# Prompt retention in tile-sized chunks with a running state on VectorE, and group normalisation applied by ScalarE

## The reference

```python
def retention_block(q, k, v, S, log_gamma):
    ...
    scores = jnp.einsum("blhd,bmhd->bhlm", q, k) * decay[None]
    intra = jnp.einsum("bhlm,bmhe->blhe", scores, v)
    ...
    cross = jnp.einsum("blhd,bhde->blhe", q, S) * q_decay[None, :, :, None]
    ...
    S_new = (jnp.exp(L * log_gamma)[None, :, None, None] * S
             + jnp.einsum("blhd,blhe->bhde", k * k_decay[None, :, :, None], v))
    return intra + cross, S_new
```

## Time and profile before

| | |
|---|---|
| time, 3 runs | 1494.13 to 1495.31 us, median 1494.76 us |
| the profiled execution's own time | 1495.21 us |
| its span in the trace | 1493.2 us |
| PE busy | 1459.1 us, 98% of the span |
| DVE busy | 1016.7 us, 68% |
| ACT busy | 615.6 us, 41% |

### The profile page before, as it was taken

The page is one execution under the profiler, slowest core; times in us unless marked ns, Lnnn a source line. Parts: engine busy times, 40 slices in busy tenths (PEclk is TensorE's granted clock), DMA queues, the critical chain, the costliest instruction groups (busy, mean ns, idle before and its releaser), DMA issues. The chain is left out here.

```text
span 1493.2 us, 29385 instructions
## 1 busy us (share of the span) xinstructions
PE 1459.1 (98%) x11053; PEld 1402.9 (94%) x11053; DVE 1016.7 (68%) x1977; ACT 615.6 (41%) x1072; POOL 43.6 (3%) x83
## 2 busy tenths in 40 slices
PE   8999999999999999999999999999999999999998
PEld 7998888999999999999999988898989999999998
DVE  5347764779998349995542777457799973699832
ACT  4223444345555115553332244444365541355411
POOL 0101100000000000000010011000000000000000
PEclk9999999999999999999999999999999999999999
DMA  4523311232333323333242143112333422333322
GB/s 143 157 70 114 95 57 54 81 97 70 86 84 95 97 75 86 100 89 97 67 141 85 57 121 92 49 56 82 85 86 85 112 78 78 85 103 95 87 86 76
DMA packets 225824, 132.72 MB, mean 89 GB/s; under 512 B 4664, under 2 KB 220656, under 8 KB 225728
## 3 DMA queue, kind: packets, MB, share of 16 engines
q1 hardware_dynamic: 220624, 114.11, 27.0%
q0 software_dynamic: 5008, 17.29, 3.8%
q10 hardware_dynamic: 96, 0.02, 0.0%
HBM read 123.23 MB, written 8.18 MB: 88 GB/s over the span
## 5 line engine op out<-in xcount | busy, mean ns | idle before, releaser
L1639 PE MATMUL ps<-act,hi_down 128*128 128x288 f32 x1408 | 245.1, 296 | 0.0
L1639 PE MATMUL ps<-mix,hi_of 128*128 128x288 f32 x1280 | 225.9, 299 | 4.8 <-DVE lo_of L983 4.2
L1771 PE MATMUL ps<-mix,hi_of 128*128 128x288 f32 x1024 | 211.3, 300 | 0.0
L1639 PEld LDWEIGHTS ps<-act,hi_down 128*128 128x128 f32 x1408 | 207.2, 189 | 0.0
L1639 PEld LDWEIGHTS ps<-mix,hi_of 128*128 128x128 f32 x1280 | 188.9, 190 | 7.8 <-issue 2.9
L1771 PEld LDWEIGHTS ps<-mix,hi_of 128*128 128x128 f32 x1024 | 162.6, 188 | 10.0 <-issue 6.6
L2044 PE MATMUL ps<-sums_b,hi_S 128*128 128x288 f32 x704 | 144.5, 298 | 9.4 <-DVE p_f L1464 8.8
L841 ACT ACTIVATE hi_S<-sum_S 128x512 fp32r<-128x512 f32 x176 | 110.0, 632 | 104.5 <-PE ps L2044 79.9
L1771 PE MATMUL ps<-mix,lo_of 128*128 128x288 f32 x512 | 150.8, 295 | 0.0
L1639 PE MATMUL ps<-act,lo_down 128*128 128x288 f32 x704 | 150.7, 296 | 0.0
L2044 PE MATMUL ps<-sums_a,hi_S 128*128 128x288 f32 x704 | 143.4, 296 | 0.0
(11 more groups left out here) (236 smaller groups left out, 2693.7 us busy)
## 6 DMA issues: line engine op xcount, KB each, us to landing
raw_of<-in_w_in SPq DMA_DIRECT2D x56, 512.0 KB, 3.7
raw_down<-in_w_down SPq DMA_DIRECT2D x32, 704.0 KB, 4.6
pair_raw<-in_w_gate SPq DMA_DIRECT2D x42, 512.0 KB, 4.0
pair_raw<-in_w_up SPq DMA_DIRECT2D x42, 512.0 KB, 5.2
raw_of<-in_w_out SPq DMA_DIRECT2D x16, 512.0 KB, 4.2
strip_even<-bias_lines POOLq DMA_DIRECT2D x8, 320.0 KB, 5.2
strip_odd<-bias_lines POOLq DMA_DIRECT2D x8, 320.0 KB, 5.5
stage<-in_x_prompt SPq DMA_DIRECT2D x4, 512.0 KB, 5.9
```

The costliest lines, as they stand in the source:

```text
L1639: last = nc.tensor.matmul(ps[:, bank + half, 0:HALF], weights(w, slot, nk)[:, k, :], src[:, k, part, HALF * half:HALF * half + HALF], star ...
L1771: last = nc.tensor.matmul(ps[:, half_bank(i), 0:HALF], weights(w, n % 2, KD)[:, k, :], mix[:, k, part, HALF * half:HALF * half + HALF], st ...
```

## The change

The prompt retention is computed in chunks of one tile. Each tile has only the score product with itself (4 full and one short per head); what comes from earlier tiles goes through a state: PE makes four separate state products (`ps[:, 3, ...]`), DVE adds them up with a decay (`running_states`), and `ret_values` adds for tiles 1 to 3 a product of decayed queries (`qd`, made by DVE in `query_decay`) with the running state `s_run`. The mask of a head shrinks to one tile and is loaded for all heads in one DMA. Key decay is the same for all prompt tiles, and ACT copies the four in one instruction. DVE makes scale `gni` and offset `gnb` of the group normalisation (`group_factors`), and ACT applies them (`group_normalise`, activation Identity); a dummy Sqrt (`sqrt_table`) is put where ACT should load that table. The order of all three engines in the stage is new.

```diff
+        dmask = place("dmask", [P, HR, 2 * P], F32, A_S2 + RING * STRIP * 4)
...
+                    c = C_KDEC + h
+                    nc.scalar.activation(kd_tok[:, h % 2, 0:QT, :], ps[:, 0, :].rearrange("p (t n) -> p t n", t=QT), ACT.Copy,
+                                         scale=cst[:, c:c + 1])
+                    nc.scalar.activation(kd_tok[0:DEC, h % 2, QT, :], ps[0:DEC, 1, 0:P], ACT.Copy,
+                                         scale=cst[0:DEC, c + HR:c + HR + 1]).then_inc(kd_evac, 1)
+
+                def group_normalise(h):
+                    eng.wait_ge(gn_inv, HR * l + h + 1)
+                    if h >= RING:
+                        eng.wait_ge(or_ps, HR * l + h - 1)
                     for t in range(TT):
-                        bank, c = (0, P * t) if t < QT else (1, 0)
-                        last = nc.scalar.activation(kd_tok[0:rows(t), h % 2, t, :], ps[0:rows(t), bank, c:c + P], ACT.Copy,
-                                                    scale=cst[0:rows(t), C_KDEC + HR * t + h:C_KDEC + HR * t + h + 1])
-                    last.then_inc(kd_evac, 1)
+                        r = rows(t)
+                        last = nc.scalar.activation(o_tok[0:r, h % 2, t, :], ret_tile(t), ACT.Identity,
+                                                    scale=gni[0:r, t:t + 1], bias=gnb[0:r, t:t + 1])
+                    last.then_inc(gn_normed, 1)
+
+                def sqrt_table():
+
+                    nc.scalar.activation(spare[:], cst[:, C_ONE:C_ONE + 1], ACT.Sqrt)
...
-                for k in range(NR + 3):
-                    h, i = k // TT, k % TT
-                    if k in AT_R:
...
+                attn_out(PAIRS - 1)
+                ret_keys(0)
+                eng.wait_ge(ka_out, 32 * l + 32)
+                for t in range(TT):
+                    tok_copy(l, 2, vr, t)
+                sqrt_table()
+                for h in range(HR):
+                    if h:
                         ret_keys(h)
...
+                        group_root(h - 1)
+                    half_unit(FIRST_R + 2 * h)
+                    if h:
+                        group_normalise(h - 1)
...
-                    if i == 2 and h >= 1:
-                        group_root(h - 1)
+                        sqrt_table()
+                for p in range(PAIRS):
+                    attn_hi(p)
+                group_root(HR - 1)
+                ret_hi(0)
+                group_normalise(HR - 1)
                 gate_silu_of(HR - 1)
+                for h in range(1, HR - 1):
+                    ret_hi(h)
+                unit_hi(FIRST_OUT + 1)
                 ret_hi(HR - 1)
-
...
+                def mask_scores(h):
+
+                    dve.wait_ge(r_ps, HR * l + h + 1)
+                    if h >= RING:
+                        dve.wait_ge(sv_done, HR * l + h - 1)
+                    nc.vector.tensor_tensor(p_ret[:, h % 2, 0:SEQ].rearrange("p (t n) -> p t n", t=QT),
+                                            ps[:, 2, :].rearrange("p (t n) -> p t n", t=QT), prompt_rows(dmask[:, h, 0:P], QT), ALU.mult)
+                    nc.vector.tensor_tensor(p_ret[0:DEC, h % 2, SEQ:TOK], ps[0:DEC, 7, SPARE:SPARE + DEC], dmask[0:DEC, h, 0:DEC],
...
+                    nc.vector.tensor_tensor(qd[:, h % 2, 0:SEQ - P].rearrange("p (t n) -> p t n", t=QT - 1),
+                                            qk_ret[:, h, P:SEQ].rearrange("p (t n) -> p t n", t=QT - 1),
+                                            prompt_rows(dmask[:, h, P:2 * P], QT - 1), ALU.mult)
+                    nc.vector.tensor_tensor(qd[:, h % 2, SEQ - P:TOK - P], qk_ret[:, h, SEQ:TOK], dmask[:, h, P:P + DEC],
...
+                def running_states(h):
+
+                    step = float(gamma(h) ** P)
+                    dve.wait_ge(st_ps, HR * l + h + 1)
+                    if h >= RING:
+                        dve.wait_ge(sv_done, HR * l + h - 1)
+                    added = [ps[:, 3, DR * t:DR * t + DR] for t in range(QT)]
+                    run = s_run[:, h % 2]
+                    done = 3 * HR * l + 3 * h
+                    nc.vector.tensor_copy(run[:, 0, :], added[0]).then_inc(s_ran, 1)
+                    for t in range(1, QT):
+                        dve.wait_ge(s_ran, done + t)
+                        dst = run[:, t, :] if t + 1 < QT else st_tmp[:, 0, :]
+                        last = nc.vector.scalar_tensor_tensor(dst, run[:, t - 1, :], step, added[t], ALU.mult, ALU.add)
+                        if t + 1 < QT:
+                            last.then_inc(s_ran, 1)
...
+                def group_factors(h):
                     dve.wait_ge(gn_root, HR * l + h + 1)
                     nc.vector.reciprocal(gni[:, 0:QT], gnr[:, 0:QT])
...
+                    nc.vector.reciprocal(gni[0:DEC, QT:TT], gnr[0:DEC, QT:TT]).then_inc(gn_recip, 1)
+                    dve.wait_ge(gn_recip, HR * l + h + 1)
+                    nc.vector.scalar_tensor_tensor(gnb[:, 0:QT], mv[:, 0:QT, 0], -1.0, gni[:, 0:QT], ALU.mult, ALU.mult)
+                    nc.vector.scalar_tensor_tensor(gnb[0:DEC, QT:TT], mv[0:DEC, QT:TT, 0], -1.0, gni[0:DEC, QT:TT],
+                                                   ALU.mult, ALU.mult).then_inc(gn_inv, 1)
...
-                for k in range(NR + 4):
-                    h, i = k // TT, k % TT
...
+                query_decay(0)
+                for h in range(HR):
+                    mask_scores(h)
+                    half_unit(FIRST_R + 2 * h)
+                    if h:
+                        group_factors(h - 1)
+                    running_states(h)
+                    if h:
+                        gated(h - 1)
+                    states(h)
+                    if h + 1 < HR:
+                        query_decay(h + 1)
+                    half_unit(FIRST_R + 2 * h + 1)
+                    if h + 1 < HR:
+                        group_stats(h)
+                for p in range(2):
+                    attn_lo(p)
+                group_stats(HR - 1)
+                for p in range(2, PAIRS):
+                    attn_lo(p)
+                group_factors(HR - 1)
+                for h in range(HR - 1):
+                    gated_lo(h)
+                unit_lo(FIRST_OUT + 1)
...
+                def ret_scores(h):
+
+                    if h:
+                        pe.wait_ge(decayed, HR * l + h)
+                        pe.wait_ge(evacuated, U_LAYER * l + U_IN - HR + h + EV)
+                    for t in range(TT):
+                        dst = ps[:, 2, tok(t)] if t < QT else ps[0:DEC, 7, SPARE:SPARE + DEC]
+                        last = nc.tensor.matmul(dst, qk_ret[:, 4 + h, tok(t)], qk_ret[:, h, tok(t)], start=True, stop=True)
...
+                        pe.wait_ge(st_sum, HR * l + h)
+                    v = vr[:, :, DR * h:DR * h + DR]
+                    for t in range(QT):
+                        last = nc.tensor.matmul(ps[:, 3, DR * t:DR * t + DR], kd_tok[:, h % 2, t, :], v[:, t, :], start=True, stop=True)
+                    last.then_inc(st_ps, 1)
...
+                def dec_states(h):
+
+                    pe.wait_ge(half_out, UNITS_H * l + UNITS_H - HR + h + 1)
+                    nc.tensor.matmul(ps[:, 6, SPARE:SPARE + DR], kd_tok[0:DEC, h % 2, QT, :], vr[0:DEC, QT, DR * h:DR * h + DR],
+                                     start=True, stop=True).then_inc(dec_st_ps, 1)
...
+                def ret_values(h):
+                    pe.wait_ge(decayed, HR * l + h + 1)
+                    pe.wait_ge(qd_ready, HR * l + h + 1)
...
+                    pe.wait_ge(s_ran, 3 * HR * l + 3 * h + 3)
...
+                        out = ps[:, 4, tok(t)]
+                        nc.tensor.matmul(out, p_ret[:, h % 2, tok(t)], v[:, t, :], start=True, stop=t == 0)
+                        if t:
+                            nc.tensor.matmul(out, qd[:, h % 2, P * (t - 1):P * t], s_run[:, h % 2, t - 1, :], start=False, stop=True)
+                    out = ps[0:DEC, 5, 0:P]
+                    nc.tensor.matmul(out, qd[:, h % 2, SEQ - P:TOK - P], s_in[:, h, :], start=True, stop=False)
+                    nc.tensor.matmul(out, p_ret[0:DEC, h % 2, SEQ:TOK], v[0:DEC, QT, :], start=False, stop=True).then_inc(sv_done, 1)
...
+                ret_scores(0)
+                to_tokens(l, 2, vt)
+                for h in range(HR):
+                    if h:
                         ret_keys(h)
-                    if k < NR:
...
+                        ret_scores(h)
+                        pe.wait_ge(st_sum, HR * l + h)
+                    else:
+                        pe.wait_ge(tok_evac, 3 * TT * l + 3 * TT - 1)
...
+                    half_unit(FIRST_R + 2 * h)
+                    if h == 0:
...
-                    if 0 <= k - 2 < NR:
-                        ret_values(k - 2)
-                    if i == TT - 1 and h >= 1:
+                    ret_states(h)
+                    if h:
                         ret_out(h - 1)
-                    if i == TT - 1 and h < HR:
```

(28 more changed lines are left out.)

182 lines of the change are left out of this document (41 added, 141 removed).

## The result

The changed kernel takes 1513.04 us in the median of four runs (1507.59 to 1515.38), the kernel before beside it 1494.45: a ratio of 1.0117, with a 95% interval of 1.009 to 1.0143. It is slower by 17.5 us by that ratio (18.6 between the medians). Forecast were 1506.0 us and a range of 1495 to 1512.5: the direction is right and the forecast is 7 us too low. The measured median lies 0.5 us above the range's upper end, and the ratio applied to the 1494.76 us of the prediction gives 1512.2, right at it.

The account below looks back on a forecast made before the run. PE, busy 98% of the span, bounds the kernel: 16.0 us of products saved, but new waits make the stage +3.3 us and clock falls add 8.0. Together +11.3 on 1495.21, 1506.5, less 0.45 for the median: 1506.0 us; range 1495 to 1512.5.

Parts of the forecast that it names:

- The products saved, 16.0 us: PE in the retention: 9 products fewer a head at 0.222 us each, 8.0 us a layer, 16.0 in all.
- The wait before `ret_out`, 2.6 us in three heads: PE, heads 1 to 3: stands 2.6 us for ACT's normalised tiles, which wait for DVE's factors; 7.8 us a layer.
- five tiles in 1.38: ACT normalises a head's five tiles in 1.38 us, taken from its five decayed copies from PSUM.
- Case C: Rival: ACT's tiles take 0.4 us each, waits grow to 3.2 us, six falls, 1512.5 us; chance 0.10.
- The wait for step 5 of the tail, 3.2 us: PE in the output projection: stands 3.2 us for DVE's low part of head 1, behind ACT's table load, silu and `ret_hi(1)`.
- The last head's operand: PE in the tail, after two steps of the second unit: waits from 12.6 until 13.0 us for head 3's operand.
- The stage at the full clock, 80.2 us: Retention stage to the third unit, a layer: 61.3 + 18.9 = 80.2 us against 78.55, +1.65 a layer, +3.3 in all.
- I take five of eight at 1.6: 8.0 us: Clock on PE: five of the stage's eight new long waits are followed by a fall costing 1.6 us each, 8.0 us.
- the one known pair: Feed-forward part, both layers: PE's waits of 2.64 us, with granted clock 0.66 in the mean of the next 5 us.
- Case D: Rival: the clock falls behind every new wait, 1498.1 + 13.6 is 1511.7 us; chance 0.13.
- Case B: Rival: DVE's factors and ACT's tiles reach `ret_out` sooner, T + 2.7 instead of T + 3.7, giving 1490.1 us; chance 0.12.
- Case F: Rival: the tail's table load holds ACT for twice its 1.28 us, 2.6 us more in all, 1508.6 us; chance 0.02.

Follow-up runs that it names:

- the first experiment: Changed kernel with DVE making the previous head's normalisation factors ahead of the evacuation of a head's first half unit, not behind it: 1479.74 us, ratio 0.9922.
- the kernel at 1473.2 us: Changed kernel with DVE's factors ahead of the half unit's evacuation and ACT's high parts of heads 0 to 2 ahead of the last head's work: 1473.17 us, ratio 0.9852.

## Why the prediction was right in direction and 7 us short

- **The products saved, 16.0 us.** Right: 144 records fewer, and 8.05 us more a layer in the stage when they were put back.
- **The wait before `ret_out`, 2.6 us in three heads.** Right in place, releaser and cause, which the first experiment shows. Its size was 3.05 in all six: of the chain's links only "five tiles in 1.38" was off. ACT's tiles with scale and offset took 1.83 us; the row taken was that of copies with a scale. Case C had the direction (0.4 a tile, 2.0), and the truth lay between.
- **The wait for step 5 of the tail, 3.2 us.** Right, 3.50, the same link. The last head's operand made no wait.
- **The stage at the full clock, 80.2 us.** 79.97: the longer waits were made up by heads that are 0.25 us shorter apart from them (12.70, in the first experiment, for 12.95) and by a tail without its last wait. So this part of the sum, +3.3 in all, stands at +2.9.
- **"I take five of eight at 1.6: 8.0 us."** This is the step that failed. All eight fell, and two of them lasted twice as long: 16.45 us. The 1.6 was right for a single fall (1.7). The count was wrong, because I read the limit as lying near 2.6 us, where the one known pair was, and took the new waits to be just under it. They were 3.05 and 3.50 us, above the pair's 2.64, so the mis-sized tiles fed this step as well; and the clock fell behind six waits of 1.93 to 2.38 us too, when they were tried, so it would not have held at 2.6. Case D was this mechanism, with 0.13 and 1511.7 us; the double falls are what it lacked. The Trainium skill (TensorE: Matmul & The Clock Gate, HAM oscillation) tells of a kernel that waited some 3 to 5 us between its bursts of matmuls, and whose clock was thrown back each time. The traces agree in the heads of the changed kernel and its variants, already for shorter waits (18 of 18 of 1.93 to 3.05 us), and not in the feed-forward part, where seven of 24 of 2.60 to 2.65 us passed.
- **The sum.** 2.9 + 16.45 is 19.35 of the 20.0 us between the two spans; the stage also began 1.57 us later (242.28 for 240.71). From the end of layer 0's stage to the start of layer 1's it took 1.1 us more (653.04 for 651.91; behind its wait of 2.60 us the clock was 0.56 over 7 us, for 0.76 before), and from there to the end 2.0 less (441.49 for 443.50; no fall behind its wait of 2.64 us, for one before). None of this was in the sum, and that it nearly cancels is luck. The profiled run is also the slowest of four, which spread over 8 us (1507.59 to 1515.38) with mean clocks of 0.988 to 0.983.
- **Case B** (the factors come early) was the right place to look for a gain, and that order, with the tail's, is the kernel at 1473.2 us. **Case F**, and the drain of 1.38 us that the Trainium skill (ScalarE: Activation LUTs, What ACT_TABLE_LOAD costs) adds to a change of table: no run shows either. A load took 1.28 us with silu right behind it, and taking the early loads away cost 4.7 us where 1.28 a load gave 4.4.

## What to carry to other kernels

An engine's list decides more than its load: DVE was 66% busy and stood idle for 2.54 us right before the chain that held PE, so look for such a pair before judging an algorithm. Price a new wait on PE twice, once as a wait and once by the granted clock behind it, and let the smallest wait that fell, not the nearest one, set the count. Where a wait can't go, fill it or make it shorter, and then look at the clock again: 0.59 us left of 3.05 was enough here, 1.93 was not.

## What the runs showed of the hardware that was not expected

- **The wait's length doesn't decide alone.** Over the profiled executions of all kernels here: in the retention heads and the tail all 20 waits of 3.05 and 3.5 us and all eight of 1.93 to 2.38 were followed by a fall. Of the 24 waits of 2.60 to 2.65 us in the feed-forward part 17 were and seven not, and the same program's two layers differed. All 26 there of 1.69 to 1.74 us were not. In the kernel with PE's order changed 3.01 and 3.03 us were not, a few us behind a fall, and one of its four of 1.57 to 1.59 was, while the four of 1.60 to 1.65 in two other kernels were not. What else counts was not tried, so no limit can be given.
- **A fall has two lengths:** 7-us windows at about 0.76, or at 0.51 to 0.58, which is 3.4 us at the lower level or about twice that. The same wait showed both: 0.52 and 0.76 for the first head in two kernels that differ only in the tail.
- **ACT's tile with scale and offset:** 1.83 us for five of 128x128 from PSUM in a row, against 1.38 for copies with a scale and DVE's 1.67.
